# Sample attention with two page buffers each for K and V instead of three

## The reference, cut to what matters

```python
def _sample_attend(q, k, v, lam, rel_bias, cache_k, cache_v, page_table):
    def one(args):
        pt, qi, ki, vi = args
        kp = cache_k[pt].reshape(past, N_ATT_HEADS, 2, ATT_HEAD_DIM)   # past = 4096
        vp = cache_v[pt].reshape(past, N_ATT_HEADS, ATT_V_DIM)
        kf = jnp.concatenate([kp, ki.astype(kp.dtype)], axis=0)
        vf = jnp.concatenate([vp, vi.astype(vp.dtype)], axis=0)
        return _diff_attention(qi[None], kf[None], vf[None], q_pos, k_pos, rel_bias, lam)[0]
    return lax.map(one, (page_table, q, k, v))

def _diff_attention(q, k, v, q_pos, k_pos, rel_bias, lam):
    s = jnp.einsum('bqhmd,bkhmd->bmhqk', q, k) * (ATT_HEAD_DIM ** -0.5)
    s = jnp.where(dist >= 0, s + bias, -jnp.inf)
    p = jax.nn.softmax(s, axis=-1)
    w = p[:, 0] - lam * p[:, 1]
    return jnp.einsum('bhqk,bkhd->bqhd', w.astype(v.dtype), v)
```

## Time and profile before

| | |
|---|---|
| median of 3 runs | 4155.42 us (4150.68 to 4158.69) |
| the profiled execution | 4143.18 us |
| its span, first to last instruction | 4141.2 us |
| mean granted TensorE clock | 0.709 of full speed |
| sample attention, first K load issued | 712.65 us |
| its last `values` matmuls end | about 1070 us |
| next stage's first load | 1089.19 us |

### The profile page before, as it was taken

How to read it: one execution, slowest core, us unless ns; L and a number is a source line. 1 busy time by engine, 2 the same in 40 slices (tenths; PEclk the granted TensorE clock), 3 DMA queues, 4 the chain that set the end, 5 groups by cost and what they waited for, 6 DMA issues and landing times. The chain is left out here.

```text
span 4141.2 us, 54520 instructions
## 1 busy us (share of the span) xinstructions
PE 2416.7 (58%) x16498; PEld 1071.3 (26%) x16498; DVE 2531.7 (61%) x6307; ACT 1399.3 (34%) x4107; POOL 1276.2 (31%) x1334
## 2 busy tenths in 40 slices
PE   5999755898695174464464455455446446446443
PEld 3446434566342021121121021112012112012110
DVE  1101254566372758758858857856866865875875
ACT  0110033333100143444434444344344344434443
POOL 0000000244100144434444434444444444443442
PEclk8999878999797585585576566567558558557555
DMA  9102341899524399999999999999999999999998
GB/s 347 51 23 62 23 1 34 352 402 415 201 98 138 139 418 421 421 405 413 421 413 410 420 405 407 421 418 407 421 415 397 421 421 402 420 420 406 409 421 345
DMA packets 245928, 1343.84 MB, mean 325 GB/s; under 512 B 47288, under 2 KB 60825, under 8 KB 94084
## 3 DMA queue, kind: packets, MB, share of 16 engines
q0 software_dynamic: 164352, 1174.49, 68.9%
q1 hardware_dynamic: 63392, 144.05, 11.0%
q10 hardware_dynamic: 17892, 21.83, 1.6%
HBM read 1319.30 MB, written 20.97 MB: 324 GB/s over the span
## 5 line engine op out<-in xcount | busy, mean ns | idle before, releaser
L1490 PE MATMUL psum<-sb_ring,sb_fold_weighted 128*32 128x256 f32 x8448 | 1030.9, 585 | 1405.1 <-PEq L62 1300.3
L1643 DVE CUSTOM_DVE_ANT_0 sb_ring<-sb_ring,sb_h_four 128x1024 f32<-128x1024 f32 x1056 | 1268.8, 1224 | 709.8 <-DMA sb_ring<-in_uv,sb_experts 676.8
L1465 POOL DMA_INDIRECT sb_ring<-in_uv,sb_experts x1056 | 1130.9, 1071 | 1758.4 <-POOLq L62 1588.1
L1490 PEld LDWEIGHTS psum<-sb_ring,sb_fold_weighted 128*32 128x32 f32 x8448 | 273.4, 136 | 2155.2 <-issue 2143.4
L1575 ACT ACTIVATE sb_gelu<-sb_dots 128x1 f32<-128x1 f32 x1056 | 210.9, 200 | 1180.9 <-ACTq L62 1175.7
L793 POOL DMA_DIRECT2D sb_v_pages<-in_cache_v x256 | 134.9, 527 | 930.6 <-issue 742.9
L1580 ACT ACTIVATE sb_fold_weighted<-sb_fold,sb_expert_w 128x32 f32<-128x32 f32 x1056 | 339.3, 321 | 34.4
L1577 ACT ACTIVATE sb_expert_w<-sb_gelu,sb_gates 128x1 f32<-128x1 f32 x1056 | 311.1, 295 | 35.0
L1508 PE MATMUL psum<-sb_w_pq,sb_h2T 128*128 128x512 f32 x576 | 321.0, 713 | 2.2 <-PEq L62 1.7
L377 PE MATMUL psum<-sb_w_qkv,sb_hT_tile 128*128 128x512 f32 (+1 forms) x432 | 187.5, 594 | 0.0
L528 PE MATMUL psum<-sb_hT,sb_w_bcu 128*128 128x352 f32 x576 | 172.9, 464 | 8.2 <-PEq L62 8.2
(11 more groups left out here) (214 smaller groups left out, 2569.0 us busy)
## 6 DMA issues: line engine op xcount, KB each, us to landing
sb_k_pages<-in_cache_k SPq DMA_DIRECT2D x256, 256.0 KB, 6.2
sb_v_pages<-in_cache_v POOLq DMA_DIRECT2D x256, 256.0 KB, 6.2
sb_w_ada<-in_w_ada SPq DMA_DIRECT2D x12, 2048.0 KB, 17.7
sb_ring<-in_uv,sb_experts POOLq DMA_INDIRECT x1056, 15.0
sb_w_pq<-in_w_pq SPq DMA_DIRECT2D x4, 2048.0 KB, 17.3
sb_w_qkv<-in_w_in SPq DMA_DIRECT2D x3, 2048.0 KB, 19.4
sb_w_bcu<-in_w_in SPq DMA_DIRECT2D x12, 512.0 KB, 6.4
sb_h_tiles<-h_scratch SPq DMA_DIRECT2D x9, 512.0 KB, 8.4
```

Source lines behind the costliest of these rows:

```text
L1465: pool.indirect_dma_start(ring[:, slot, :], None, uv, bass.IndirectOffsetOnAxis(ap=experts[:, u, g, n:n + 1], axis=0))\
L1490: ins = nc.tensor.matmul(psum[q * NS:(q + 1) * NS, g % 2, 0:QUARTER], fw[:, slot, :], ring[:, slot, D + q * QUARTER:D + (q + 1) * QUARTER] ...
L1643: dot = nc.vector.tensor_tensor_reduce(ring[:, slot, 0:D], ring[:, slot, 0:D], h2x[:, g % 2], 1.0, 0.0, ALU.mult, ALU.add, dots[:, slot:sl ...
```

## The change

`DEEP` goes from 3 to 2. With it the tiles `k_pages` and `v_pages` have two slots instead of three, the semaphores `k_land`, `k_free`, `v_land` and `v_free` are two of each kind, and the numbers waited for follow from k // DEEP.

```diff
@@ -742,7 +742,7 @@ def sample_attention
     CH = 4
     NCH = PAGES // CH
     STEPS = NB * NCH
-    DEEP = 3
+    DEEP = 2
     WROW = 2 + AW + NB * NS
```

## The result

The changed kernel takes 4202.15 us (median of 5 runs, 4184.34 to 4206.34) against 4154.11 us for the kernel before (5 runs): a ratio of 1.0107, 95% interval 1.0083 to 1.0131, or +35 to +54 us. The forecast was +12 us, its range up to +37. The stage itself tells the same: from the first K load to the next stage's first load (SP at L1163) it was 1089.19 - 712.65 = 376.5 us, and is now 1139.86 - 723.86 = 416.0 us, +39.5.

What follows compares the result with a forecast made beforehand. The prediction took PE to bound the kernel, with DMA 1.5% behind. Start +3, settled part +6 and end +3 summed to +12 us, added to the median 4155.42 for 4167.4 us; range +2 to +37, 4157 to 4192.

Steps and rivals of the forecast that it cites:

- rival B: Every round is bound by the load: +24 us, 4179, or +55 us, 4210; requests 43.5 us or more apart; chance 0.18.
- Start, +3, between +1 and +4: First loads: four chunks asked for ahead of the first transpose instead of six, so early chunks come later; +3 us.
- Settled part, +6: Steps between start and end: a K slot's round slightly too long, +0.1 us a step over 57 steps, +6 us.
- a round with 8.0 us: K slot's round with 8.0 us from first issue to next transposes: 10.64 us, or 5.32 a step.
- allowance of 7.6 us: Most time a K load may take from first issue to next transposes within a round of 10.26 us without loss.
- chunk 6 (+0.31): K load taking 8.24 us from issue to transposes: round of 10.88 us, 5.44 a step, +18 us.
- chunk 9 (+0.86): K load taking 9.33 us from issue to transposes: round of 11.97 us, 5.99 a step, +49 us.
- So K decides: Settled part: the K slot's round, not the V slot's, sets the pace, since V's allowance is looser.
- V is looser by 0.9: `values` hold a V slot only 1.06 us, so a V load may take 8.5 us, against 7.6 for K.
- End, +3: V loads 62 and 63 wait for `values` of chunks 60 and 61, so the last `values` come later; +3 us.
- Rival C, the clock: Waits for pages drop PE to half clock; in half the steps that gives +147 us, 4303 us; chance 0.03.
- The rule of a fixed cost plus the bytes: A DMA takes about 2.0 us plus bytes at 436 GB/s: K load 4.5 us, settled part costs nothing.

Runs made afterwards that it cites:

- k3v2: The kernel before with two V slots instead of three, K kept at three; ratio 1.0054 to the kernel before.
- ends2: The kernel before, three slots each, but load 2 and the last two loads of each kind wait as with two slots; ratio 1.0031 to the kernel before.
- k4v4: The kernel before with four K and four V slots instead of three each; ratio 0.9975 to the kernel before.
- onedma: The changed kernel with each load one 1 MB DMA from four consecutive pages instead of four DMAs; ratio 1.0042 to the kernel before.
- halfv: The changed kernel loading only two of four V pages per chunk from chunk 2 on; ratio 1.0055 to the kernel before.
- nov: The changed kernel without V loads from chunk 2 on; ratio 1.0009 to the kernel before.
- onequeue: The changed kernel with one 1 MB DMA per load, consecutive pages, K and V both issued by SP, no page numbers read; ratio 0.9980 to the kernel before.

## Why the prediction was wrong

The mechanism was right in the main: the loads wait for slots, PE waits for pages, and start, settled part and end all lose. The size was not. By the prediction's own signs rival B is what happened: requests 45.58 us apart, where it named 43.5 or more for B, and a price of +24 to +55 us. By its steps:

- *Start, +3, between +1 and +4.* Chunk 2 was turned at 752.16 - 723.86 = 28.3 us after the first load, against 27.7 and 24.9 in the two profiles before; the wait just before it was 3.08 us. Chunk 7 was turned 57.3 and 58.1 us after the first load in the two profiles of the changed kernel, 52.7 and 52.6 in those of the kernel before: +4.6 to +5.5, so the forecast for the start was too small by about 2 us. A part of it is that transposes there ran at the lower clock (2.63 us for those of chunk 2).
- *Settled part, +6; the step that failed.* "I take the pace halfway between no loss and a round with 8.0 us." This puts the time from a K load's first issue to the next transposes at about 7.8 us, halfway between 7.6 and 8.0. In the changed kernel it was 8.92 us (mean over chunks 16 to 55). The other two parts of the round were near what the prediction had (2.03 of transposes against 1.97, 0.45 to the issue against 0.67); with the 8.92 they make the measured round of 11.4 us, 5.70 a step. Halving the loss was a guess at how far fewer loads in the queues relieve each other. The load did fall, from 8.78 to 7.67 us until its last packet, but from there to the transposes another 1.25 pass on average. And the allowance of 7.6 us came from the mean step (5.13), though the earlier trace rows shows 4.8 for an ordinary one. Measured: +0.57 a step, +22.6 over chunks 16 to 56 and about +26 to the last transposes, where 0.1 a step and +6 were forecast. It lies halfway between the values worked out for chunk 6 (+0.31) and chunk 9 (+0.86).
- *"So K decides", "V is looser by 0.9".* Wrong: k3v2 loses 21.6 us by V alone. The prediction allowed a V load 8.5 us from its issue to `values`; in k3v2 it took 9.0 (mean over chunks 16 to 55).
- *End, +3.* It was +7.7. Near its last loads POOL is late once by more than its pace, and now has no slot to hide it:

```profile
1104.96 2.26 POOL L793 DMA_DIRECT2D sb_v_pages<-in_cache_v  x4 [3.50 <-PE psum L883]
1112.47 2.27 POOL L793 DMA_DIRECT2D sb_v_pages<-in_cache_v  x4 [5.25 <-issue]
```
```profile
1110.96 1.24 PE L883 MATMUL psum<-sb_v_pages,sb_probsT 128*8 128x128 f32 x32 [0.85 <-DMA sb_v_pages<-in_cache_v]
1118.75 1.67 PE L883 MATMUL psum<-sb_v_pages,sb_probsT 128*8 128x128 f32 x26 [6.55 <-DMA sb_v_pages<-in_cache_v]
```

  The slot for load 63 was free at about 1107.6, POOL's own pace of 4.53 us would have had it out at 1109.5, and it went at 1112.47: 3 us of the 4.7 that are missing. Another 1.1 is the way from that issue to the last `values` (6.28 instead of 5.21 us), and these ran at the lower clock: all 32 of them took 1.90 us instead of 1.06 (the row above holds 26 of them). A delay of this kind stood in the earlier trace rows, as the 5.50 before load 62, and I charged only the pace behind it. It stands before load 62 in the second profile of the kernel before (5.50), before load 63 with two V slots (5.25 in the changed kernel, 5.26 in k3v2), before load 62 in ends2 (13.12) and before load 61 in k4v4 (5.39), and not in onedma. It also stands once in the middle of the stage, before load 32 of V, first in the kernel before, then in the changed one:

```profile
905.81 2.27 POOL L793 DMA_DIRECT2D sb_v_pages<-in_cache_v  x4 [5.57 <-issue]
```
```profile
935.29 2.27 POOL L793 DMA_DIRECT2D sb_v_pages<-in_cache_v  x4 [6.96 <-issue]
```

  Before, the third slot hides it: PE doesn't wait for V there. With two V slots PE waits for chunk 32 each time: 2.56 us in the changed kernel (943.26, below), 3.97 in its second profile, 3.60 in k3v2. So a few of the 22.6 us of the settled part are POOL's delay. It comes at nearly the same two places of POOL's program in every kernel that issues four V loads a chunk; its cause no run here tests.
- *Rival C, the clock.* It came, but small. Some windows show 0.96 (one of the second profile 0.92), and single rows show it: the transposes of chunk 5 took 3.21 us after a wait of 3.05, those of chunk 36 took 3.50 instead of 1.94, after a wait of 2.56 for V.

```profile
769.84 3.21 PE L835 MATMUL psum<-sb_ident,sb_k_pages 128*128 128x128 f32 x16 [3.05 <-DMA sb_k_pages<-in_cache_k]
...
943.26 1.06 PE L883 MATMUL psum<-sb_v_pages,sb_probsT 128*8 128x128 f32 x32 [2.56 <-DMA sb_v_pages<-in_cache_v]
944.65 3.50 PE L835 MATMUL psum<-sb_ident,sb_k_pages 128*128 128x128 f32 x16 [0.33 <-PE psum L883]
```

  Each time it adds 1.3 to 1.6 us. Of the settled part it can be little: a window of 41 us at 0.96 lacks 0.04 x 41 = 1.6 us of full clock, and there are two such windows between chunks 16 and 56. halfv, at 1.00 throughout these chunks, lost 2.4 us a request all the same. The Trainium skill, "TensorE: Matmul & The Clock Gate", section "HAM oscillation — how this bites in real kernels", tells of the same kind of loss: DMA waits between groups of matmuls, after which the next group runs at the lower of PE's two clock levels.
- *The rule of a fixed cost plus the bytes* (the Trainium skill, "DMA: Bandwidth & Descriptors", section "Anatomy of one DMA — SWDGE (gpsimd) path"). It would have given no loss in the settled part. The page gives it per DMA on the gpsimd path and says nothing there of loads in company, "whatever else is queued" is my reading of it; the K loads are issued by SP. In nov, without V, there was indeed no loss, though a page took 3.4 us against the rule's 2.6. Beside V (4.9 us) there was one, so the rule failed where it would have decided.

What stays open: the share of jitter. If PE began each time as soon as it could, the changed kernel's round would be 1.95 + 0.2 to 0.7 + 7.67 + 0.5 = 10.3 to 10.8 us, 5.2 to 5.4 a step, and 5.70 was measured. Most of the difference is in the 1.25 us between last packet and transposes, where 0.5 would do: in part of the steps the page was there before PE came. So single long loads (up to 9.2 us), POOL's late issues and PE's own long steps can each hold up the round; since chunks are used in order, a late one delays the next as well and an early one helps nobody. What each of them costs, and that they add up so, is argued, not shown.

## What to carry to other kernels

Count a buffer's round, not the average rates: time held by the consumer, way to the issue, load as it takes in company, and way back, against as many ordinary steps of the consumer as there are buffers. Here two buffers did where that held for the short steps and the slower loads (nov), and not where it held only on average or for some loads (halfv, the changed kernel). Where a third is absent, late issues and long loads that it would have hidden are paid for. Where the room for a third is missing, loads in one DMA instead of four, kept in one queue in the order of their use, gave back here what the third slot was worth; these runs read consecutive pages, and a kernel with a page table would have to try it.

## What the runs showed of the hardware

- Loads of 256 KB, issued four in about 2 us, landed 3.4 us after their issue (median) without a second stream, 4.9 us with two 1 MB buffers of a second stream and 6.5 with three of both, at rates of 205 to 209, 360 to 387 and 401 to 415 GB/s (nov, the changed kernel and the kernel before, 850 to 1014 us).
- Half the V traffic (about 290 GB/s in all) still lengthened the K load by 1.2 us, far from the full rate (halfv against nov, 6.89 against 5.69).
- Two engines' queues with loads of 1 MB in each had them land after 8.1 and 8.6 us (onedma). The same loads issued by one engine into one queue landed after 7.5 and 7.4 (onequeue), at a higher total rate: 408 to 411 against 373 to 396 GB/s. Whether the queue or the issuing engine makes the difference is not told apart.
- POOL issued load 32 of V, and again one of the loads 61 to 63, 5.3 to 13.1 us after its last issue without a wait that the profile shows, in every kernel that issued four V loads a chunk.
